# The inverse of an RWKV recurrence: two heads in one 128x128 block, or each head as its own 64x64 product

## The chip, the core and the metric

The kernel runs on one core of a Trainium2 chip. The core has TensorE (PE, matrix products into PSUM, with its weight loads shown apart as PEld), VectorE (DVE), ScalarE (ACT), GpSimd (POOL) and SyncE (SP, which issues transfers). The engines run their own instruction streams and meet at semaphores. The metric is the device time of one launch in microseconds (us), less is better.

## The reference

One inference step of a hybrid recurrent decoder in fp32: 512 prompt tokens and 8 sample tokens go through an even layer (RG-LRU and RWKV-7, dense SwiGLU, gated embedding) and an odd layer (Mamba-2 SSD and GLA, top-2-of-8 mixture of experts, gated embedding). The part that matters here is the RWKV-7 recurrence of the prompt, 8 heads of 64x64:

```
def step(S, inp):
    r_t, k_t, v_t, d_t, kk_t, a_t = inp
    S = (S * d_t[:, :, None, :]
         - einsum('bhvk,bhk->bhv', S, kk_t)[..., None] * (kk_t * a_t)[:, :, None, :]
         + v_t[..., None] * k_t[:, :, None, :])
    return S, einsum('bhvk,bhk->bhv', S, r_t)
```

## The kernel before

The step is not run token by token. The 512 tokens are cut into 8 chunks of 64. Inside a chunk each head needs the inverse of a unit lower triangular 64x64 matrix, identity plus a strictly triangular A. Heads are held in pairs: 4 pairs (t), the first head of a pair on partitions 0 to 63, the second on 64 to 127 (hh). The recurrence block (lines 655 to 876) makes four passes, s = 0 to 3, of two chunks each (cc), so that a pass inverts 8 pairs (n = 4 cc + t), 16 matrices.

Before the change a pair is one block-diagonal 128x128 matrix. AL holds A (L605), with zeros off the diagonal blocks, set once by GpSimd (L664). DD is the inverse so far, EE its transpose (DVE's transpose works in 32x32 blocks, which is enough up to the fourth level), OO the part of A that the next level takes in, GG a product on its way.

A pass has three pieces.

- Head: PE writes A by 64x64 products into the diagonal quarters of `ps0` (L740, `ab_mm`), then the products for the output (L747, into `ps1` and `ps2`), then transposes (L755, L763). DVE copies A out of PSUM (L835, two copies), masks it (L837), forms identity minus mask (L838), transposes it (L839), masks A for the first level (L842), and then masks the output products (L847, `am_read`). ScalarE copies the transposes out (L801, L805).
- Five levels l = 0 to 4, each in two groups of four pairs (cc, the chunks). PE forms G = OO' EE (L778), ScalarE copies G (L811), PE forms the correction (L784, at the last level L786), DVE subtracts it from DD (L854) and transposes DD into EE (L855); at the last level it subtracts from EE (L858) and nothing follows. GpSimd masks A for the next level (L670, `next_o`) as soon as G is out.
- The recurrence over the two chunks (`recur`, L698), small products whose first ones stand at L678 and L688. It waits for the last subtraction (`de_read`).

Of the kernel before, what the change touches and what calls it, by code (L numbers as in the profile page):

```python
# [17 lines left out]
ALU = mybir.AluOpType  # L18
# [3 lines left out]
P = 128  # L22
# [84 lines left out]
def build_program(nc, i, o):  # L107

    with ExitStack() as ctx:
# [510 lines left out]
        names = ("ab_mm", "ab_read", "am_mm", "am_read", "bk_mm", "bk_read", "v_mm", "v_read", "d_ready", "e_ready",  # L620
# [30 lines left out]
        def nth(s, l, cc):  # L651

            return 10 * s + 2 * l + cc + 1

        with nc.Block() as block:
            @block.sync
            def _(sp):
                loaded.on(sp.dma_start(Dm[:, 0:961], i["ph_rw"]), 16)  # L658

            @block.gpsimd  # L660
            def _(pool):
                S = Serial(pool, pool_step)
                pool_step.on(pool.memset(B[0:64, 10240:11264], 0.0))
                S(pool.memset(u_sb[:, 0:1024], 0.0))  # L664
                for s in range(4):
                    for l in range(4):
                        for cc in range(2):
                            n = slice(4 * cc, 4 * cc + 4)
                            w(pool, "g_mm", nth(s, l, cc))
                            g["next_o"].on(pool.tensor_tensor(OO[:, n], AL[:, n], spread(level(l + 2), 4, 1), ALU.mult))  # L670

            @block.tensor
            def _(pe):
# [24 lines left out]
                def recur(c, cc):  # L698
# [32 lines left out]
                for s in range(4):  # L731
                    if s:
                        w(pe, "de_read", 10 * s)
                        w(pe, "z_read", 4 * s)
                        w(pe, "y_read", 2 * s)
                    for cc in range(2):
                        for t in range(4):
                            n = (4 * cc + t) * P
                            for hh in range(2):
                                mm = pe.matmul(ps[0][64 * hh:64 * hh + 64, n + 64 * hh:n + 64 * hh + 64],  # L740
# [25 lines left out]
                    w(pe, "d_ready", s + 1)  # L766
                    w(pe, "am_read", 2 * s + 2)
                    w(pe, "v_read", s + 1)  # L768
                    for l in range(5):
                        for cc in range(2):  # L770
                            if l == 0:
                                w(pe, "o_ready", 2 * s + cc + 1)  # L772
                                w(pe, "e_ready", s + 1)  # L773
                            else:
                                w(pe, "next_o", 8 * s + 2 * (l - 1) + cc + 1)
                                w(pe, "de_read", nth(s, l - 1, cc))
# [3 lines left out]
                        for cc in range(2):  # L780
                            w(pe, "g_read", nth(s, l, cc))
                            for n in range(4 * cc, 4 * cc + 4):
                                if l < 4:
                                    mm = pe.matmul(ps[1][:, n * P:(n + 1) * P], GG[:, n, :], DD[:, n, :], start=True, stop=True)  # L784
                                else:
                                    mm = pe.matmul(ps[2][:, n * P:(n + 1) * P], DD[:, n, :], GG[:, n, :], start=True, stop=True)  # L786
                            g["eg_mm"].on(mm)
                    w(pe, "de_read", 10 * s + 10)
# [5 lines left out]
            def _(act):  # L794
                for s in range(4):
# [10 lines left out]
                    for l in range(5):  # L806
                        for cc in range(2):
                            w(act, "g_mm", nth(s, l, cc))
                            if l:
                                w(act, "eg_mm", nth(s, l - 1, cc))  # L810
                            g["g_read"].on(act.activation(u_sb[:, 3072 + 512 * cc:3584 + 512 * cc],  # L811
                                                          ps[0][:, 512 * cc:512 * cc + 512], ACT.Copy))
# [14 lines left out]
            def _(dve):  # L827
                S = Serial(dve, dve_step)
                dve.wait_ge(loaded.sem, loaded.count)
                dve.wait_ge(pool_step.sem, pool_step.at(2))  # L830
                for s in range(4):
                    w(dve, "ab_mm", s + 1)
                    for hh in range(2):
                        j = 64 * hh
                        S(dve.tensor_copy(AL[j:j + 64, :, j:j + 64], pairs(ps[0][j:j + 64, :])[:, :, j:j + 64]),  # L835
                          g["ab_read"] if hh else None)
                    S(dve.tensor_tensor(OO, AL, spread(level(0), 8, 1), ALU.mult))  # L837
                    S(dve.tensor_tensor(DD, spread(ident, 8, 1), OO, ALU.subtract), g["d_ready"])  # L838
                    S(dve.transpose(u_sb[:, 2048:3072], u_sb[:, 1024:2048]), g["e_ready"])  # L839
                    for cc in range(2):  # L840
                        n = slice(4 * cc, 4 * cc + 4)
                        S(dve.tensor_tensor(OO[:, n], AL[:, n], spread(level(1), 4, 1), ALU.mult), g["o_ready"])  # L842
# [6 lines left out]
                    for l in range(5):  # L849
                        for cc in range(2):  # L850
                            n, half = slice(4 * cc, 4 * cc + 4), slice(512 * cc, 512 * cc + 512)
# [1665 lines left out]
```

## Time and profile before

| | |
|---|---|
| median of 3 runs | 2316.57 us (2315.2 to 2317.98) |
| the profiled execution, its time | 2314.37 us |
| its span, first to last instruction | 2312.6 us |
| PE busy, PEld busy | 2034.9 us (88%), 1801.2 us (78%) |
| DVE, ACT, POOL busy | 648.3 us (28%), 368.1 us (16%), 154.1 us (7%) |
| mean granted clock | 0.93 of 2.4 GHz |
| recurrence block | some 185 us, from 218.8 to 404 |

The busy shares are means over the whole program. The large matrix products with streamed weights make most of it; the recurrence block is 8% of the span, and in it the shares are different, so it has to be read by itself. The granted clock is 1.00 or 0.50, that is 2.4 or 1.2 GHz; values between are means over a stretch.

### The profile page before, as it was taken

Reading aid. Unit: us, or ns where it says so; the run is one execution under the profiler, and the core shown is the slowest. Engines: PE = TensorE matmul, PEld = TensorE weight load, DVE = VectorE, ACT = ScalarE, POOL = GpSimd, SP = SyncE. Lnnn points to the kernel's source line nnn. Section 1 sums busy time; section 2 is a strip of 40 time slices with the busy share of each in tenths; the row PEclk is TensorE's granted clock in tenths of the full one; section 3 lists DMA queues with packets and bytes.
Section 4 is the critical chain, followed back from the end, with each engine's and each line's share of the span. In section 5 each row is a group of like instructions: output and inputs, shape, how many; then the busy total and the mean of one; then the engine's idle time right before and its main releaser. Section 6 shows DMA issues by size and latency. Waiting matters only on the chain. (4 is left out here: it accounts for less than half of the span.)

```text
span 2312.6 us, 31395 instructions
## 1 busy us (share of the span) xinstructions
PE 2034.9 (88%) x12810; PEld 1801.2 (78%) x12810; DVE 648.3 (28%) x991; ACT 368.1 (16%) x716; POOL 154.1 (7%) x171
## 2 busy tenths in 40 slices
PE   6987777598999999998999776859999999999677
PEld 5876666277888888876888454759999999999566
DVE  4378555722000000023620666220000000000053
ACT  1553222100000000011231111110111110111121
POOL 0001221503000000000000200010000000000100
PEclk9999999899999999999999766959999999999878
DMA  4111000118322222222222200048878878877520
GB/s 158 64 55 55 1 1 2 41 56 334 129 76 78 73 88 75 71 75 79 73 73 73 89 19 21 19 149 274 280 254 269 271 264 277 284 258 264 218 75 37
DMA packets 73824, 292.20 MB, mean 126 GB/s; under 512 B 8513, under 2 KB 9665, under 8 KB 72465
## 3 DMA queue, kind: packets, MB, share of 16 engines
q1 hardware_dynamic: 61920, 249.68, 31.8%
q0 software_dynamic: 7904, 28.46, 3.2%
q10 hardware_dynamic: 3920, 12.93, 1.6%
q8 instruction: 58, 0.95, 0.2%
q14 instruction: 22, 0.17, 0.0%
HBM read 255.50 MB, written 35.54 MB: 126 GB/s over the span
## 5 line engine op out<-in xcount | busy, mean ns | idle before, releaser
L190 PE MATMUL ps<-normed,ring 128*128 128x260 f32 (+1 forms) x3424 | 763.6, 385 | 16.7 <-DVE normed L233 16.7
L190 PEld LDWEIGHTS ps<-normed,ring 128*128 128x128 f32 (+1 forms) x3424 | 652.1, 191 | 125.4 <-issue 22.9
L2167 PE MATMUL ps<-proj,ring 128*128 128x144 f32 x3168 | 392.9, 287 | 3.5 <-DVE proj L2250 3.1
L2167 PEld LDWEIGHTS ps<-proj,ring 128*128 128x128 f32 x3168 | 391.0, 191 | 4.3 <-DVE proj L2250 3.8
L2184 PE MATMUL ps<-temps,ring 128*128 128x144 f32 x1584 | 200.5, 286 | 0.0
L2184 PEld LDWEIGHTS ps<-temps,ring 128*128 128x128 f32 x1584 | 197.2, 190 | 0.0
L190 PE MATMUL ps<-proj,ring 128*128 128x260 f32 x640 | 151.1, 397 | 18.4 <-PEq L904 8.5
L190 PEld LDWEIGHTS ps<-proj,ring 128*128 128x128 f32 x640 | 126.7, 199 | 40.9 <-issue 14.1
L190 PE MATMUL ps<-wide,ring 128*128 128x260 f32 x704 | 154.6, 383 | 0.9 <-DVE wide L1214 0.9
L190 PEld LDWEIGHTS ps<-wide,ring 128*128 128x128 f32 x704 | 133.7, 190 | 21.8 <-DVE wide L1214 1.3
L2243 DVE TENSOR_TENSOR temps<-temps,ps 128x144 f32<-128x144 f32 x99 | 30.2, 305 | 361.6 <-PE ps L2167 324.6
L1214 DVE TENSOR_TENSOR wide<-temps,ps 128x520 f32 (+1 forms) x22 | 15.3, 696 | 291.9 <-PE ps L190 291.9
L778 PE MATMUL ps<-normed,temps 128*128 128x128 f32 x320 | 50.8, 312 | 43.5 <-DVE temps L847 26.3
L778 PEld LDWEIGHTS ps<-normed,temps 128*128 128x128 f32 x320 | 44.8, 218 | 49.1 <-issue 49.1
L208 ACT ACTIVATE temps<-resid 128x520 f32<-128x520 f32 (+1 forms) x56 | 34.6, 632 | 291.6 <-DVE resid L1223 158.3
L2215 ACT ACTIVATE temps<-ps 128x144 f32<-128x144 f32 x99 | 28.8, 291 | 310.2 <-PE ps L2167 310.1
L2245 DVE COPY proj<-ps 128x512 f32<-128x512 f32 x9 | 6.2, 692 | 205.2 <-PE ps L2110 205.2
L1193 ACT ACTIVATE temps<-ps 128x520 f32<-128x520 f32 x22 | 13.3, 604 | 294.4 <-PE ps L190 294.4
L2282 POOL DMA_INDIRECT wide<-rows_y,slot_of x10 | 9.3, 934 | 645.0 <-SPq L2273 642.3
L2218 ACT ACTIVATE proj<-ps 128x144 f32<-128x144 f32 x72 | 21.0, 291 | 190.6 <-PE ps L2184 190.6
L670 POOL TENSOR_TENSOR temps<-normed,phase 128x512 f32<-128x512 f32 x32 | 40.6, 1270 | 128.0 <-PE ps L778 128.0
L190 PE MATMUL ps<-temps,consts 128*128 128x260 f32 x28 | 13.0, 609 | 38.8 <-PEq L262 15.9
(441 smaller groups left out, 1616.9 us busy)
## 6 DMA issues: line engine op xcount, KB each, us to landing
ring<-in_w_moe_gu SPq DMA_DIRECT2D x198, 512.0 KB, 4.3
ring<-in_w_moe_dn SPq DMA_DIRECT2D x72, 704.0 KB, 5.8
ring<-in_w_gu SPq DMA_DIRECT2D x44, 512.0 KB, 3.5
ring<-in_w_in_cd SPq DMA_DIRECT2D x25, 512.0 KB, 3.5
ring<-in_w_in_ab SPq DMA_DIRECT2D x22, 512.0 KB, 3.5
ring<-in_w_dn SPq DMA_DIRECT2D x16, 704.0 KB, 4.0
ring<-in_w_ple SPq DMA_DIRECT2D x16, 640.0 KB, 4.0
rows_x<-proj POOLq DMA_DIRECT2D x18, 512.0 KB, 11.1
```

The source lines that it names most:

```text
L190: mm = pe.matmul(dst[0:width, a:a + HALF], slab[:, k * width:(k + 1) * width], x[:, a:a + HALF], start=first and k == 0, stop=last and k = ...
L208: act.activation(SQ_SUM if m == 0 else sq_tmp(m), h3[:, m, :] if src is None else src, ACT.Square).then_inc(sq_done.sem, 1)
L670: g["next_o"].on(pool.tensor_tensor(OO[:, n], AL[:, n], spread(level(l + 2), 4, 1), ALU.mult))
L778: mm = pe.matmul(ps[0][:, n * P:(n + 1) * P], OO[:, n, :], EE[:, n, :], start=True, stop=True)
L1193: act.activation(tmp2(m), pt(2 * (m % 2)), ACT.Silu).then_inc(silu_done.sem, 1)
L1214: dve.tensor_tensor(dst, tmp2(m), pt(2 * (m % 2) + 1), ALU.mult).then_inc(hid_done.sem, 1)
L2167: mm = pe.matmul(hid_psum(m, s), slot(Q_MOE + 2 * m + s)[:, f * P:(f + 1) * P], XT[:, f, :], start=f == 0, stop=f == KD - 1)
L2184: mm = pe.matmul(down_psum(m), slot(Q_MOE + 2 * KE + m)[:, f * P:(f + 1) * P], HK(f), start=f == 0, stop=f == KE - 1)
L2215: act.activation(TMPH(m), hid_psum(m, 0), ACT.Silu).then_inc(silu_done.sem, 1)
L2218: act.activation(YT[:, m, :], down_psum(m), ACT.Copy).then_inc(yt_cp.sem, 1)
L2243: dve.tensor_tensor(HK(m), TMPH(m), hid_psum(m, 1), ALU.mult).then_inc(hid_done.sem, 1)
L2282: gather_in[tt].on(pool.indirect_dma_start(out=dst[0:w, :], out_offset=None, in_=rows_y[:, :], in_offset=at), 16)
```

## The change

Each head becomes a product of its own on a quarter of the array. AL, DD, EE, GG and OO hold 64 columns a pair instead of 128: head 0 on partitions 0 to 63, head 1 on 64 to 127, both in the same columns, and no zeros. `by_head` issues for each pair two 64x64 products, from partitions 0 to 63 into 0 to 63 and from 64 to 127 into 64 to 127. The masks come with 64 columns (577 columns in place of 961). The copy of A is one instruction, the memset of AL goes, and all DVE, ScalarE and GpSimd instructions on these tiles have half the columns. There are still two groups of four pairs a level (GROUPS = 2). The signal `d_ready` goes, and PE's wait for `am_read` moves behind the G products of level 0.

The diff, without the renaming of cc to gr in the waits:

```diff
-        rwmask, level = Dm[:, 0:P], lambda l: Dm[:, P * (1 + l):P * (2 + l)]
-        sign, i64 = Dm[:, 7 * P:7 * P + 1], Dm[:, 7 * P + 1:7 * P + 65]
+        rwmask, level = Dm[:, 0:P], lambda l: Dm[:, P + 64 * l:P + 64 * (l + 1)]
+        sign, i64 = Dm[:, 512:513], Dm[:, 513:577]
-        AL, DD, EE, GG = [pairs(u_sb[:, n * 1024:(n + 1) * 1024]) for n in range(4)]
-        OO = pairs(C[:, 0:1024])
+        heads = lambda ap: ap.rearrange("p (n c) -> p n c", c=64)
+        AL, DD, EE, GG = [heads(u_sb[:, n * 512:(n + 1) * 512]) for n in range(4)]
+        OO = heads(C[:, 0:512])
+        GROUPS = 2
+        PER_G = 8 // GROUPS
+        members = lambda gr: slice(PER_G * gr, PER_G * (gr + 1))
+        gcols = lambda base, gr: slice(base + 64 * PER_G * gr, base + 64 * PER_G * (gr + 1))
...
+        def nth(s, l, gr):
+
+            return GROUPS * (5 * s + l) + gr + 1
+
+        def g_psum(gr):
+            return ps[0][:, 512 * gr:512 * gr + 64 * PER_G]
+
+        def d_psum(gr, l):
+            return ps[1 if l < 4 else 2][:, 512 * gr:512 * gr + 64 * PER_G]
+
+        def by_head(pe, dst, lhs, rhs, gr):
+
+            for n in range(PER_G):
+                for hh in range(2):
+                    j = slice(64 * hh, 64 * hh + 64)
+                    mm = pe.matmul(dst[j, 64 * n:64 * n + 64], lhs[j, PER_G * gr + n, :], rhs[j, PER_G * gr + n, :],
+                                   start=True, stop=True)
+            return mm
...
-                loaded.on(sp.dma_start(Dm[:, 0:961], i["ph_rw"]), 16)
+                loaded.on(sp.dma_start(Dm[:, 0:577], i["ph_rw"]), 16)
...
-                S(pool.memset(u_sb[:, 0:1024], 0.0))
...
-                            g["next_o"].on(pool.tensor_tensor(OO[:, n], AL[:, n], spread(level(l + 2), 4, 1), ALU.mult))
+                            g["next_o"].on(pool.tensor_tensor(OO[:, n], AL[:, n], spread(level(l + 2), PER_G, 1), ALU.mult))
...
-                                               EE[j:j + 64, 4 * cc + t, j:j + 64], Qs[j:j + 64, t, :],
+                                               EE[j:j + 64, 4 * cc + t, :], Qs[j:j + 64, t, :],
...
-                                mm = pe.matmul(ps[0][64 * hh:64 * hh + 64, n + 64 * hh:n + 64 * hh + 64],
+                                mm = pe.matmul(ps[0][64 * hh:64 * hh + 64, n:n + 64],
...
-                    w(pe, "d_ready", s + 1)
-                    w(pe, "am_read", 2 * s + 2)
                     w(pe, "v_read", s + 1)
                     for l in range(5):
...
-                            for n in range(4 * cc, 4 * cc + 4):
-                                mm = pe.matmul(ps[0][:, n * P:(n + 1) * P], OO[:, n, :], EE[:, n, :], start=True, stop=True)
-                            g["g_mm"].on(mm)
...
+                            g["g_mm"].on(by_head(pe, g_psum(gr), OO, EE, gr))
+                        if l == 0:
+                            w(pe, "am_read", 2 * s + 2)
+                        for gr in range(GROUPS):
+                            w(pe, "g_read", nth(s, l, gr))
+                            lhs, rhs = (GG, DD) if l < 4 else (DD, GG)
+                            g["eg_mm"].on(by_head(pe, d_psum(gr, l), lhs, rhs, gr))
...
-                            g["g_read"].on(act.activation(u_sb[:, 3072 + 512 * cc:3584 + 512 * cc],
-                                                          ps[0][:, 512 * cc:512 * cc + 512], ACT.Copy))
+                            g["g_read"].on(act.activation(u_sb[:, gcols(1536, gr)], g_psum(gr), ACT.Copy))
...
-                dve.wait_ge(pool_step.sem, pool_step.at(2))
...
-                    for hh in range(2):
-                        j = 64 * hh
-                        S(dve.tensor_copy(AL[j:j + 64, :, j:j + 64], pairs(ps[0][j:j + 64, :])[:, :, j:j + 64]),
-                          g["ab_read"] if hh else None)
+                    S(dve.tensor_copy(AL, heads(ps[0][:, 0:512])), g["ab_read"])
                     S(dve.tensor_tensor(OO, AL, spread(level(0), 8, 1), ALU.mult))
-                    S(dve.tensor_tensor(DD, spread(ident, 8, 1), OO, ALU.subtract), g["d_ready"])
-                    S(dve.transpose(u_sb[:, 2048:3072], u_sb[:, 1024:2048]), g["e_ready"])
+                    S(dve.tensor_tensor(DD, spread(i64, 8, 1), OO, ALU.subtract))
+                    S(dve.transpose(u_sb[:, 1024:1536], u_sb[:, 512:1024]), g["e_ready"])
...
-                                S(dve.tensor_tensor(DD[:, n], DD[:, n], pairs(ps[1][:, half]), ALU.subtract))
-                                S(dve.transpose(u_sb[:, 2048 + 512 * cc:2560 + 512 * cc],
-                                                u_sb[:, 1024 + 512 * cc:1536 + 512 * cc]), g["de_read"])
+                                S(dve.tensor_tensor(DD[:, n], DD[:, n], heads(d_psum(gr, l)), ALU.subtract))
+                                S(dve.transpose(u_sb[:, gcols(1024, gr)], u_sb[:, gcols(512, gr)]), g["de_read"])
                             else:
-                                S(dve.tensor_tensor(EE[:, n], EE[:, n], pairs(ps[2][:, half]), ALU.subtract), g["de_read"])
+                                S(dve.tensor_tensor(EE[:, n], EE[:, n], heads(d_psum(gr, l)), ALU.subtract), g["de_read"])
```

What stands on PE between the head's transposes and the second level, before (`normed` holds AL, DD, EE and GG, `temps` holds OO, `wide` the chunk's operands):

```order
L763 MATMUL ps<-consts,wide 128x64 x15
L778 MATMUL ps<-normed,temps 128x128 [waits rw_o_ready,rw_v_read,rw_e_ready,rw_am_read,rw_d_ready]
L778 MATMUL ps<-normed,temps 128x128 x3
L778 MATMUL ps<-normed,temps 128x128 [waits rw_e_ready,rw_o_ready]
L778 MATMUL ps<-normed,temps 128x128 x3
L784 MATMUL ps<-normed 128x128 [waits rw_g_read]
L784 MATMUL ps<-normed 128x128 x3
L784 MATMUL ps<-normed 128x128 [waits rw_g_read]
L784 MATMUL ps<-normed 128x128 x3
L778 MATMUL ps<-normed,temps 128x128 [waits rw_de_read,rw_next_o]
```

And after the change (L671 is the product in `by_head`, L782 the same transposes as L763):

```order
L782 MATMUL ps<-consts,wide 128x64 x15
L671 MATMUL ps<-normed,temps 64x64 [waits rw_e_ready,rw_o_ready,rw_v_read]
L671 MATMUL ps<-normed,temps 64x64 x7
L671 MATMUL ps<-normed,temps 64x64 [waits rw_e_ready,rw_o_ready]
L671 MATMUL ps<-normed,temps 64x64 x7
L671 MATMUL ps<-normed 64x64 [waits rw_g_read,rw_am_read]
L671 MATMUL ps<-normed 64x64 x7
L671 MATMUL ps<-normed 64x64 [waits rw_g_read]
L671 MATMUL ps<-normed 64x64 x7
L671 MATMUL ps<-normed,temps 64x64 [waits rw_de_read,rw_next_o]
```

The wait for `am_read` has moved from the first G product to the first correction product, two groups later, and each group has 8 products instead of 4.

On DVE the head of a pass, before:

```order
L835 COPY normed<-ps 64x8x64 [waits dve_step]
L837 TENSOR_TENSOR temps<-normed,phase 128x1024 [waits rw_ab_read]
L838 TENSOR_TENSOR normed<-consts,temps 128x1024 [waits dve_step]
L839 STREAM_TRANSPOSE normed<-normed 128x1024 [waits rw_d_ready]
L842 TENSOR_TENSOR temps<-normed,phase 128x512 [waits rw_e_ready]
L842 TENSOR_TENSOR temps<-normed,phase 128x512 [waits rw_o_ready]
L847 TENSOR_TENSOR temps<-ps,phase 128x1024 [waits rw_am_mm,rw_o_ready]
L847 TENSOR_TENSOR temps<-ps,phase 128x1024 [waits rw_am_mm,rw_am_read]
L854 TENSOR_TENSOR normed<-normed,ps 128x512 [waits rw_eg_mm,rw_am_read]
```

And after:

```order
L844 COPY normed<-ps 128x512 [waits rw_ab_mm,loaded]
L845 TENSOR_TENSOR temps<-normed,phase 128x512 [waits rw_ab_read]
L846 TENSOR_TENSOR normed<-phase,temps 128x512 [waits dve_step]
L847 STREAM_TRANSPOSE normed<-normed 128x512 [waits dve_step]
L850 TENSOR_TENSOR temps<-normed,phase 128x256 [waits rw_e_ready]
L850 TENSOR_TENSOR temps<-normed,phase 128x256 [waits rw_o_ready]
L855 TENSOR_TENSOR temps<-ps,phase 128x1024 [waits rw_am_mm,rw_o_ready]
L855 TENSOR_TENSOR temps<-ps,phase 128x1024 [waits rw_am_mm,rw_am_read]
L862 TENSOR_TENSOR normed<-normed,ps 128x256 [waits rw_eg_mm,rw_am_read]
```

The order is the same but for one copy that went; the widths are halved on all but the two maskings of the output products (L847 before, L855 after).

## Rows read from the trace of the kernel before

**Rows 1.** a stage: length, busy us of PE, PEld, DVE, ACT, POOL, clock, DMA
```profile
264.50:310.00 45.50, 32.81 (x454) 30.61 (x452) 24.96 (x39) 10.40 (x23) 10.16 (x8) 0.92 0.01 1
```

**Rows 2.** timeline, head of pass s=1: start, length, engine, instruction, idle before
```profile
266.21 1.15 PE L740 MATMUL ps<-wide 64*64 64x64 f32 x32 [0.68 <-DVE phase L874]
267.46 1.41 DVE L835 COPY normed<-ps 64x512 f32<-64x512 f32 x2 [1.35 <-PE ps L740]
271.01 1.02 ACT L805 ACTIVATE wide<-ps 64x1024 f32<-64x1024 f32 x1
271.43 1.25 DVE L839 STREAM_TRANSPOSE normed<-normed 128x1024 f32<-128x1024 f32 x1
272.71 1.42 DVE L842 TENSOR_TENSOR temps<-normed,phase 128x512 f32<-128x512 f32 x2
274.16 2.48 DVE L847 TENSOR_TENSOR temps<-ps,phase 128x1024 f32<-128x1024 f32 x2
276.75 3.55 PE L778 MATMUL ps<-normed,temps 128*128 128x128 f32 x16 [6.41 <-DVE temps L847]
281.29 0.69 DVE L854 TENSOR_TENSOR normed<-normed,ps 128x512 f32<-128x512 f32 x1 [4.65 <-PE ps L784]
```

**Rows 3.** timeline, one level of pass s=0
```profile
238.63 0.71 DVE L855 STREAM_TRANSPOSE normed<-normed 128x512 f32<-128x512 f32 x1
239.46 0.97 PEld L778 LDWEIGHTS ps<-normed,temps 128*128 128x128 f32 x8 [0.50 <-issue]
240.34 1.93 PEld L784 LDWEIGHTS ps<-normed 128*128 128x128 f32 x16
241.62 0.69 DVE L854 TENSOR_TENSOR normed<-normed,ps 128x512 f32<-128x512 f32 x1 [2.28 <-PE ps L784]
242.34 0.71 DVE L855 STREAM_TRANSPOSE normed<-normed 128x512 f32<-128x512 f32 x1
```

**Rows 4.** timeline, tail of pass s=0
```profile
257.14 0.69 DVE L858 TENSOR_TENSOR normed<-normed,ps 128x512 f32<-128x512 f32 x1 [2.28 <-PE ps L786]
258.84 0.69 PE L678 MATMUL ps<-wide,temps 128*64 128x64 f32 x16 [0.85 <-DVE normed L858]
```

**Rows 5.** groups by shape: count, busy us, mean ns, idle before; then two timeline rows
```profile
L740 PE MATMUL ps<-wide 64*64 64x64 f32 x128 | 5.4, 243 | 6.3 <-PEq L362 4.3 <-DVE phase L874 2.0
L740 PEld LDWEIGHTS ps<-wide 64*64 64x64 f32 x128 | 4.9, 156 | 7.0 <-issue 7.0
L873 DVE TENSOR_TENSOR phase<-ps,phase 128x128 f32<-128x128 f32 x14 | 4.1, 292 | 9.3 <-PE ps L720 9.0
L855 DVE STREAM_TRANSPOSE normed<-normed 128x512 f32<-128x512 f32 x32 | 22.8, 711 | 1.1
L823 ACT ACTIVATE proj<-ps 128x256 f32<-128x256 f32 x8 | 3.1, 384 | 8.1 <-PE ps L725 8.1
L670 POOL TENSOR_TENSOR temps<-normed,phase 128x512 f32<-128x512 f32 x32 | 40.6, 1270 | 128.0 <-PE ps L778 128.0
...
262.38 0.68 PE L688 MATMUL ps<-phase,wide 64*64 64x64 f32 x16
262.83 0.55 PEld L695 LDWEIGHTS ps<-wide,phase 64*64 64x64 f32 x16
```

**Rows 6.** timeline, head of pass s=0
```profile
218.90 1.97 PE L740 MATMUL ps<-wide 64*64 64x64 f32 x32 [4.28 <-PEq L362]
222.17 1.41 DVE L835 COPY normed<-ps 64x512 f32<-64x512 f32 x2 [3.82 <-DMA phase<-in_ph_rw]
236.44 0.69 DVE L854 TENSOR_TENSOR normed<-normed,ps 128x512 f32<-128x512 f32 x1 [5.09 <-PE ps L784]
```

**Rows 7.** granted clock of short stretches, and PE around its fall at 416
```profile
272.00:274.00 2.00, 0.00 (x0) 0.00 (x0) 1.93 (x3) 0.03 (x1) 0.00 (x0) 0.78 0.00 0
416.70:418.40 1.70, 1.70 (x4) 0.67 (x3) 1.31 (x2) 0.95 (x2) 0.00 (x0) 0.50 0.00 0
...
415.55 5.40 PE L921 MATMUL ps<-normed,consts 128*128 128x512 f32 x8 [2.17 <-POOL normed L979]
```

More of the change, by code:

```diff
@@ L618, in rk @@
             return B[64 * hh:64 * hh + 64, j:j + 64 * n]
-        names = ("ab_mm", "ab_read", "am_mm", "am_read", "bk_mm", "bk_read", "v_mm", "v_read", "d_ready", "e_ready",
+        names = ("ab_mm", "ab_read", "am_mm", "am_read", "bk_mm", "bk_read", "v_mm", "v_read", "e_ready",
                  "o_ready", "next_o", "g_mm", "g_read", "eg_mm", "de_read", "q_mm", "q_read", "p_mm",
@@ L663, in _ @@
                 pool_step.on(pool.memset(B[0:64, 10240:11264], 0.0))
-                S(pool.memset(u_sb[:, 0:1024], 0.0))
                 for s in range(4):
                     for l in range(4):
-                        for cc in range(2):
-                            n = slice(4 * cc, 4 * cc + 4)
-                            w(pool, "g_mm", nth(s, l, cc))
-                            g["next_o"].on(pool.tensor_tensor(OO[:, n], AL[:, n], spread(level(l + 2), 4, 1), ALU.mult))
+                        for gr in range(GROUPS):
+                            n = members(gr)
+                            w(pool, "g_mm", nth(s, l, gr))
+                            g["next_o"].on(pool.tensor_tensor(OO[:, n], AL[:, n], spread(level(l + 2), PER_G, 1), ALU.mult))
             @block.tensor
@@ L732, in _ @@
                     if s:
-                        w(pe, "de_read", 10 * s)
+                        w(pe, "de_read", 5 * GROUPS * s)
                         w(pe, "z_read", 4 * s)
@@ L806, in _ @@
                     for l in range(5):
-                        for cc in range(2):
-                            w(act, "g_mm", nth(s, l, cc))
+                        for gr in range(GROUPS):
+                            w(act, "g_mm", nth(s, l, gr))
                             if l:
-                                w(act, "eg_mm", nth(s, l - 1, cc))
-                            g["g_read"].on(act.activation(u_sb[:, 3072 + 512 * cc:3584 + 512 * cc],
-                                                          ps[0][:, 512 * cc:512 * cc + 512], ACT.Copy))
+                                w(act, "eg_mm", nth(s, l - 1, gr))
+                            g["g_read"].on(act.activation(u_sb[:, gcols(1536, gr)], g_psum(gr), ACT.Copy))
                     for cc in range(2):
@@ L849, in _ @@
                     for l in range(5):
[L850 to L852 removed]
+                        for gr in range(GROUPS):
+                            n = members(gr)
+                            w(dve, "eg_mm", nth(s, l, gr))
                             if l < 4:
[L854 to L856 removed]
+                                S(dve.tensor_tensor(DD[:, n], DD[:, n], heads(d_psum(gr, l)), ALU.subtract))
+                                S(dve.transpose(u_sb[:, gcols(1024, gr)], u_sb[:, gcols(512, gr)]), g["de_read"])
                             else:
[L858 removed]
+                                S(dve.tensor_tensor(EE[:, n], EE[:, n], heads(d_psum(gr, l)), ALU.subtract), g["de_read"])
                     for cc in range(2):
@@ L2378, in shape_constants @@
         ti, si = r[:, None], r[None, :]
-        levels.append(((ti // (2 * m) == si // (2 * m)) & ((ti // m) % 2 == 1) & ((si // m) % 2 == 0)).astype(np.float32))
+        levels.append(((ti // (2 * m) == si // (2 * m)) & ((ti // m) % 2 == 1) & ((si // m) % 2 == 0)).astype(np.float32)[:, 0:64])
+        levels[-1][64:] = levels[-1][:64]
     sign = np.where(np.arange(P) < 64, -1.0, 1.0).astype(np.float32)[:, None]
```

30 lines of the change are left out of this document (10 added, 20 removed).

## The prediction

> **What bounds the kernel now.** I first read the busy time by stage [rows 1]. The RWKV recurrence runs as four passes (s = 0 to 3) of some 45.5 us each. In the second, TensorE (PE) works 32.8 us and VectorE (DVE) 25.0 us out of 45.5: neither is full, so the stage is a chain that goes back and forth between them, and an instruction only counts if it lies on that chain. The timeline shows the chain in three pieces.
>
> The head of a pass [rows 2]: PE starts its small products at 266.21, DVE can start at 267.46, and from there it works without a hole: two copies out of PSUM (1.41), a mask and identity minus mask (from 268.87 to 271.43, 1.28 each with their gaps), transpose (1.25), two masks (1.42), two maskings of the 1024-wide products (2.48). The first inverse product waits for the last of them (releaser DVE L847) and starts at 276.75. The first subtraction L854 comes at 281.29, 13.83 after DVE's start.
>
> One level [rows 3]: the second group's transpose ends at 239.34, PE loads that group's G product at 239.46 (0.12 later), starts the first group's EG product at 240.34 (0.88 later), DVE subtracts at 241.62 (1.28 later: the product's end and a handover of 0.05), then four DVE operations (0.69, 0.71, 0.69, 0.71 and three gaps of 0.03) end 2.89 later, and the next level's second G product follows. 0.12 + 0.88 + 1.28 + 2.89 = 5.17, which is the distance of two levels: the first subtractions stand at 236.44 [rows 6] and 241.62, 5.18 apart. ScalarE's copy of G and GpSimd's mask are done earlier and only have to keep up.
>
> The tail [rows 4]: from the last level's first subtraction (257.14) to the recurrence's first product (258.84) 1.70.
>
> **The change, part by part.** Every operation of the inverse works on 64 columns a head pair instead of 128. What each costs:
>
> DVE, rows of before at several widths: an operation of this kind out of PSUM takes 292 ns at 128 columns [rows 5] and 0.69 us at 512 [rows 3], so 1.04 ns a column and 0.43 at 256. A transpose takes 0.711 at 512 [rows 5] and 1.25 at 1024 [rows 2], so 0.44 at 256 on the same line. A mask at 512 takes 0.69 (two with a gap 1.42 [rows 2]). The copy of AL is one in place of two (0.70 instead of 1.41). Bounds: no 256-wide operation of these kinds is in the trace; half of the 512-wide time (0.34 and 0.36) is the least, the full 512-wide time the most; I take the line, since two points support it. Four operations with three gaps of 0.03 then last 0.43 + 0.44 + 0.43 + 0.44 + 0.09 = 1.83, not 2.89.
>
> ScalarE: a 128x256 copy out of PSUM is in the trace, 384 ns [rows 5]. GpSimd: 1270 ns at 512 [rows 5]; at 256 it lies between half and all of that. Even at all of it two masks (2.5 us) fit into the level of 3.15 worked out below; at the 0.9 that I expect there is 1 us to spare.
>
> PE: a group is no longer 4 products of 128x128 on the whole array (8 records) but 8 of 64x64, alternating between two opposite quarters (16 records). The trace has exactly this form: L740, with the same two quarters, into one bank, 32 records in 1.15 at the full clock [rows 2]. Two such groups of 16 records in the recurrence start 0.46 apart (262.38, 262.83) and one needs 0.68 to its end [rows 5]. So a group takes 0.46 to issue (was 0.88) and 0.69 + 0.05 from its first load to DVE's start (was 1.28).
>
> Whether the two quarters really overlap decides this price. If they took turns, a record would cost half of a full 128-column one, 0.88 / 8 / 2 = 55 ns; L740 shows 1.15 / 32 = 36 ns at most, and the recurrence 0.46 / 16 = 29 ns. I take 29 and keep 55 as a rival. The Trainium skill, "TensorEngine Tiling (Array Packing)", section "Restrictions and Gotchas", says that different row tiles cannot use one PSUM bank at the same time; both row halves write one bank here, so by that rule they would take turns, and the trace does not agree for this diagonal pair of quarters.
>
> One level is then 0.12 + 0.46 + 0.74 + 1.83 = 3.15. EG waits for nothing new: the first group's G starts 0.81 before the second's transpose ends, is out 0.12 before that end, and its copy ends 0.30 after it, while EG is issued 0.58 after it. Saved: 5.17 - 3.15 = 2.02 a level, four levels a pass, 8.08.
>
> Head: DVE's row from its start to am_read is 0.70 + 0.69 + 0.69 + 0.71 + 2 x 0.43 + 2.48 + 6 x 0.03 = 6.31. The wait for am_read now stands behind the first G products, so these run under DVE's two large maskings. They wait for ScalarE's copy of v (L805, ends 272.03 [rows 2]) and would start at 272.15; both copies of G are out by 273.8, about when am_read comes (267.46 + 6.31 = 273.77). Then 0.11 and 0.74 to the first subtraction: 7.16 in place of 13.83, saved 6.67. This move is where I cost the G products of level 0 and their copies at nothing: the maskings hide them; without that cover they would cost 1.2. The same two maskings (2.48) are late next, unchanged by this edit.
>
> Tail: the second EG group starts when its G is copied, 1.28 in my count from the transpose's end, is out at 2.02, subtracted at 2.45; the recurrence starts at 2.56, 1.24 after the first subtraction (1.32). Saved 1.70 - 1.24 = 0.46.
>
> First pass: DVE starts at 222.17 on the table's transfer and subtracts at 236.44 [rows 6], 14.27 later; 7.16 saves 7.11. The table shrinks from 961 to 577 columns; DVE can start no sooner than L740's end (218.90 + 1.97 = 220.87), so the gain is between 0 and 1.25; I take 0.7, by the 40% fewer bytes. GpSimd's memset of 1024 columns goes, for nothing: it ended before DVE's start.
>
> Sum: three passes at 6.67 + 8.08 + 0.46 = 15.21 are 45.6, the first 7.11 + 0.7 + 8.08 + 0.46 = 16.35: 62.0 saved.
>
> **The clock.** Ahead of L778 at 276.75 PE was idle for 6.41 [rows 2]; the granted clock fell from 2.4 to 1.2 GHz in that wait (0.78 in the stretch 272 to 274, so at about 273.1 [rows 7]), and the first 16 records took 3.55, where 16 at the full clock are loaded in 1.93 [rows 3]. That loss sits in the head that the change shortens, where PE's wait shrinks from 6.41 to some 1.8 us (it ends at 272.15 instead of 276.75). But a wait of 2.17 behind L979 was also followed by a fall: 0.50 in the stretch 416.7 to 418.4 [rows 7]. So some passes will still see 1.2 GHz after the head. Price: L740 at half clock takes 1.97 for 1.15 [rows 2, 6], a group 0.36 more to issue and about 0.5 more to its end: 0.87 more a level, and two levels and a little run so, some 2.2. Of the four passes I count one to two: 3 us.
>
> The profiled execution took 2314.37, its span 2312.6, so 1.8 lies around it, unchanged. 2314.37 - 62.0 + 3 = 2255.4. The median of the runs shown, 2316.57, is 2.2 higher; I lean a little to it: **2256**.
>
> **Rivals.**
> (A) The forecast, 2249 to 2262: 0.70.
> (B) The new products run slower in every level: they take turns (55 ns a record), or the clock does not hold at 2.4 GHz under products on quarters. Both give a group of some 0.88: level 0.12 + 0.88 + 1.15 + 1.83 = 4.0, 0.85 more in each of 16 levels, 3 more in heads and tails: 2252.4 + 13.6 + 3 = 2269. Against: L740, and the recurrence, which runs on quarters at full clock. For: PE's waits between groups are a larger share of 3.15 than of the recurrence. 0.12.
> (C) DVE's operations do not shrink with the columns: at the 512-wide time a level is 3.15 + 1.06, 17 us in all, 2271. For: no 256-wide row. Against: the line through other widths. 0.05.
> (D) The gain is given back downstream: the next block starts earlier and waits there. Its transfers are issued in the block itself, and weights come through a ring that moves with PE, so I find no fixed time to wait for; 2275 to 2316. 0.04. That it is all given back, so no change: 0.01 of it.
> (E) More is saved: no falls of the clock, smaller DVE times, down to 2245: 0.06.
> (F) Slower than before. Each quarter's weight load waits for the other quarter's product to end, since the array changes tile at every instruction: a load (156 ns) and a product (243 ns) one behind the other [rows 5] are 0.40 a record, 6.4 a group, 5.7 more. Ten groups a pass lie in series (one in the head, two a level, one in the tail), 40 x 5.7 = 228: 2252 + 228 = 2480. It decides from 62 / 40 = 1.55 more a group, some 126 ns a record; L740 shows at most 36. 0.03.
>
> About 0.2% (5 us) is what a measurement of this kernel can tell from no change. Faster: A, B, C, E and most of D, 0.96; same 0.01; slower 0.03. The range 2247 to 2268 holds A, nearly all of E and part of B.
>
> **What would show it.** Level to level, the first subtractions 3.15 apart (4.0 under B or C; then PE's record spacing or DVE's durations tell which). The first subtraction 7.2 after DVE's AL copy. DVE TENSOR_TENSOR at 128x256 0.42 and transpose 0.44, ScalarE 0.38, GpSimd under 1.27. Groups of 16 records in 0.55 of loads. Granted clock 1.00 in most of the levels. The passes some 30 us apart instead of 45.3. If the L854-like subtraction waits for GpSimd's mask or for ScalarE's copy instead, my chain is wrong.

## The result and the profile after

The changed kernel takes 2257.34 us (median of 4, 2255.17 to 2259.21), the kernel before in the same runs 2317.28 (2315.20 to 2318.14). The ratio is 0.9742, 95% interval 0.9725 to 0.9759. The prediction was 2256, range 2247 to 2268. The profiled execution took 2255.17 against 2314.37, its span is 2253.3 against 2312.6.

All of the 59.3 us of the span lies in the recurrence block. It lasted from the first A product to the next block's first transfer 404.17 - 218.90 = 185.27; now 344.80 - 219.44 = 125.36, 59.9 less. It starts 0.5 later, and what follows it lasts 1908.4 before and 1908.5 now. The busy times of the second pass, from the view by stage, in the columns of [rows 1]:

```profile
250.90:282.70 31.80, 25.44 (x608) 23.14 (x608) 17.33 (x38) 8.25 (x22) 5.77 (x8) 0.89 0.01 2
```

The pass is 31.8 long instead of 45.5 (from the first copy of one pass to that of the next the passes take 30.2, 31.8 and 30.6; the profile of before has 45.3, 45.5 and 46.5); PE gave up 7.4 of busy time and DVE 7.6, so most of what a pass lost was chain, not the work of one engine.

The head of that pass, from the timeline, against [rows 2]:

```profile
250.99 1.15 PE L759 MATMUL ps<-wide 64*64 64x64 f32 x32 [0.68 <-DVE phase L881]
...
252.25 0.69 DVE L844 COPY normed<-ps 128x512 f32<-128x512 f32 x1 [1.36 <-PE ps L759]
...
255.17 0.89 DVE L850 TENSOR_TENSOR temps<-normed,phase 128x256 f32<-128x256 f32 x2
255.80 1.02 ACT L818 ACTIVATE wide<-ps 64x1024 f32<-64x1024 f32 x1
256.09 2.48 DVE L855 TENSOR_TENSOR temps<-ps,phase 128x1024 f32<-128x1024 f32 x2
...
256.87 1.15 PE L671 MATMUL ps<-normed,temps 64*64 64x64 f32 x32 [1.75 <-ACT wide L818]
...
258.63 1.97 PE L671 MATMUL ps<-normed 64*64 64x64 f32 x32 [0.61 <-DVE temps L855]
...
259.86 0.42 DVE L862 TENSOR_TENSOR normed<-normed,ps 128x256 f32<-128x256 f32 x1 [1.29 <-PE ps L671]
...
263.92 0.42 DVE L862 TENSOR_TENSOR normed<-normed,ps 128x256 f32<-128x256 f32 x1 [2.23 <-PE ps L671]
```

The G products start at 256.87 on ScalarE's copy of v, while DVE still masks; the correction products start at 258.63 when DVE is done. The 32 records of G take 1.15, the 32 of the correction 1.97: the clock fell between them, and the next first subtraction comes 4.06 later instead of the 3.24 of a level at the full clock.

One level at the full clock, in the first pass, against [rows 3], and the tail of that pass against [rows 4]:

```profile
230.88 0.45 DVE L863 STREAM_TRANSPOSE normed<-normed 128x256 f32<-128x256 f32 x1
...
231.45 0.57 PEld L671 LDWEIGHTS ps<-normed,temps 64*64 64x64 f32 x16 [0.36 <-issue]
...
231.91 1.27 PEld L671 LDWEIGHTS ps<-normed 64*64 64x64 f32 x32
...
232.73 0.42 DVE L862 TENSOR_TENSOR normed<-normed,ps 128x256 f32<-128x256 f32 x1 [1.40 <-PE ps L671]
...
235.97 0.42 DVE L862 TENSOR_TENSOR normed<-normed,ps 128x256 f32<-128x256 f32 x1 [1.40 <-PE ps L671]
...
242.44 0.42 DVE L865 TENSOR_TENSOR normed<-normed,ps 128x256 f32<-128x256 f32 x1 [1.40 <-PE ps L671]
...
243.62 0.69 PE L697 MATMUL ps<-wide,temps 128*64 128x64 f32 x16 [0.59 <-DVE normed L865]
```

Transpose ends 231.33, load 231.45 (0.12), next group 231.91 (0.46), first subtraction 232.73 (0.82), and DVE's four operations end 1.84 after that: 3.24 a level, and the next first subtraction stands at 235.97. The tail is 1.18. The groups by shape (mean ns behind the busy time), against [rows 5]:

```profile
L689 POOL TENSOR_TENSOR temps<-normed,phase 128x256 f32<-128x256 f32 x32 | 23.1, 726 | 88.8 <-PE ps L671 88.6
L824 ACT ACTIVATE normed<-ps 128x256 f32<-128x256 f32 x40 | 15.3, 384 | 47.5 <-PE ps L671 47.2
L863 DVE STREAM_TRANSPOSE normed<-normed 128x256 f32<-128x256 f32 x32 | 14.2, 445 | 1.1
L862 DVE TENSOR_TENSOR normed<-normed,ps 128x256 f32<-128x256 f32 x32 | 13.5, 421 | 22.7 <-PE ps L671 22.2
```

### The profile page after: what moved, and what is told of

It is laid out like the page before. It is cut to its first block and busy times, and to the rows that moved or that the text cites. A ratio compares the mean times of both kernels' runs of the same rounds, so it can differ in the third digit from the quotient of the medians.

```text
span 2253.3 us, 32669 instructions
## 1 busy us (share of the span) xinstructions
PE 1998.1 (89%) x13450; PEld 1763.9 (78%) x13450; DVE 617.9 (27%) x987; ACT 359.3 (16%) x716; POOL 135.9 (6%) x170
## 5 line engine op out<-in xcount | busy, mean ns | idle before, releaser
L1230 DVE TENSOR_TENSOR resid<-ps,resid 128x520 f32 (+1 forms) x8 | 5.6, 700 | 146.8 <-PE ps L190 146.8
L671 PE MATMUL ps<-normed,temps 64*64 64x64 f32 x640 | 27.6, 230 | 18.2 <-DVE normed L863 11.2
L671 PEld LDWEIGHTS ps<-normed,temps 64*64 64x64 f32 x640 | 23.6, 141 | 22.3 <-issue 14.7
```

The source lines that it names most:

```text
L671: mm = pe.matmul(dst[j, 64 * n:64 * n + 64], lhs[j, PER_G * gr + n, :], rhs[j, PER_G * gr + n, :], start=True, stop=True)
```

## The experiments

The theory is the chain account of the prediction: head, levels and tail, each the sum of PE's groups and DVE's operations on the way. The rivals are that one engine's part makes the whole gain; that the move of the wait is worth nothing; that the quarters do not overlap, or cost the clock. Each kernel ran in three rounds beside the kernel before. The block's length, read as above in each kernel's profiled execution, takes out what happens elsewhere. The last column is the distance of two levels' first subtractions while the clock is at 2.4 GHz.

| kernel | median us | ratio to before (95%) | block us | level, full clock |
|---|---|---|---|---|
| before | 2317.28 | 1 | 185.3 | 5.17 |
| changed | 2257.34 | 0.9742 (0.9725 to 0.9759) | 125.4 | 3.24 |
| E1 wait back in front | 2261.44 | 0.9767 (0.9751 to 0.9784) | 131.1 | 3.24 |
| E2 before, wait moved | 2302.76 | 0.9946 (0.9929 to 0.9962) | 173.5 | 5.17 |
| E3 quarter after quarter | 2269.72 | 0.9805 (0.9789 to 0.9821) | 138.1 | 3.60 |
| E4 one group a level | 2313.03 | 0.9986 (0.9976 to 0.9995) | 181.5 | not seen |
| E5 before, products on quarters | 2305.21 | 0.9958 (0.9944 to 0.9972) | 173.4 | 4.30 |
| E6 shorter head | 2250.76 | 0.9716 (0.9700 to 0.9732) | 119.4 | 3.24 |
| E7 before, half the products | 2370.92 | 1.0237 (1.0220 to 1.0255), see below | 172.8 | 4.28 to 4.29 |
| E8 products twice | 2277.43 | 0.9831 (0.9814 to 0.9847) | 144.1 | 4.17 |
| E9 maskings in the levels | 2247.09 | 0.9704 (0.9688 to 0.9720) | 117.4 | 3.24 |

### E1 and E2: what the move of the wait is worth

```diff
+                    w(pe, "am_read", 2 * s + 2)
                     w(pe, "v_read", s + 1)
                     for l in range(5):
...
-                        if l == 0:
-                            w(pe, "am_read", 2 * s + 2)
```

> The changed kernel, with PE's wait for am_read put back ahead of the G products of level 0. Theory (the wait's move pays because DVE's two large maskings hide the first G products and their copies): the first subtraction comes 6.31 + 0.11 + 1.16 (G product, copy, handovers) + 0.82 = 8.40 after DVE's AL copy starts instead of 7.18, 1.2 more a pass, 4.9 in all; PE's wait grows to 3.5 us, so the granted clock falls in more passes, 0 to 4 us more. 2262 to 2266. Rival (the G products are hidden anyway, the move is worth nothing): no change, 2257.

```profile
261.49 1.97 PE L671 MATMUL ps<-normed,temps 64*64 64x64 f32 x32 [3.51 <-DVE temps L854]
```

E2 is the opposite edit in the kernel before.

> The kernel before, with the wait for am_read moved behind the G products of level 0 and nothing else. Theory: the first G products start some 3.2 us sooner, at half clock since PE has been idle, and the first correction product starts when am_read comes, so the first subtraction is 2.0 to 3.0 sooner in each pass: 8 to 12 us less, 2306 to 2309. Rival (most of the gain of the head comes from halved columns, the move alone gives nothing): 2317.

E1's median is 4.1 above the changed kernel's, by the ratios 5.8, and its block is 5.7 longer. The first subtraction comes 8.75 to 9.32 after the AL copy, against 7.18 to 7.63. That is more than the 8.40 expected: PE now waits 3.51 in three of the four heads (the row above is from the second), and in every head one set of 32 records takes 1.92 to 1.97 where it takes 1.15 at the full clock. The rival of no change is out. The median came just under the stated 2262 to 2266.

E2 took 2302.76, 12.6 us less than the kernel before beside it and less than the 2306 to 2309 expected. Its head (pass s=1):

```profile
265.78 1.41 DVE L836 COPY normed<-ps 64x512 f32<-64x512 f32 x2 [1.36 <-PE ps L740]
...
271.98 3.50 PE L777 MATMUL ps<-normed,temps 128*128 128x128 f32 x16 [3.32 <-DVE temps L843]
...
275.27 2.14 PE L785 MATMUL ps<-normed 128*128 128x128 f32 x16
...
276.63 0.69 DVE L855 TENSOR_TENSOR normed<-normed,ps 128x512 f32<-128x512 f32 x1 [1.67 <-PE ps L785]
```

G starts at 271.98, 6.20 after the copy where it was 9.29 in [rows 2], so 3.0 of its 3.50, at half clock, run under the maskings (to 274.96), and the corrections behind it already run at the full clock (2.14 for 16 records and their end). The first subtraction comes after 10.85 instead of 13.83. So the wait alone, in the old widths, is worth a fifth of the whole gain. In the new widths it is worth 4 to 6 us: there G takes 1.15 and not 3.50, so there is less to hide. The parts do not simply add.

### E3: do the two quarters overlap?

```diff
-            for n in range(PER_G):
-                for hh in range(2):
+            for hh in range(2):
+                for n in range(PER_G):
```

> The changed kernel, but a group's 8 products run first all four in one quarter, then all four in the other, instead of alternating. Theory (the quarters overlap when they alternate; a record alone takes half of a full one, 55 ns): a group takes 0.88 instead of 0.46 to issue and 0.42 more to its end, a level 3.24 + 0.84 = 4.08, 13.4 us in 16 levels and 2 more in heads and tails: 2273. Rival (records are bound by issue at 29 ns whatever quarter they use): no change, 2257.

```profile
234.93 0.42 DVE L862 TENSOR_TENSOR normed<-normed,ps 128x256 f32<-128x256 f32 x1 [1.76 <-PE ps L671]
...
237.46 0.19 PEld L671 LDWEIGHTS ps<-normed 64*64 64x64 f32 x2
...
237.51 0.14 PEld L671 LDWEIGHTS ps<-normed,temps 64*64 64x64 f32 x1
...
237.57 0.14 PEld L671 LDWEIGHTS ps<-normed 64*64 64x64 f32 x1
...
237.63 1.52 PEld L671 LDWEIGHTS ps<-normed 64*64 64x64 f32 x29
...
238.53 0.42 DVE L862 TENSOR_TENSOR normed<-normed,ps 128x256 f32<-128x256 f32 x1 [1.76 <-PE ps L671]
```

In this timeline the last 29 loads of a level take 1.52, 52 ns each, changes of quarter among them. A short window on the loads of one quarter shows what a record costs there alone:

```profile
236.94 0.25 PEld L671 LDWEIGHTS ps<-normed,temps 64*64 64x64 f32 x3
```

Three loads of 0.135 each span 0.25, so they start 58 ns apart; the prediction put 55 on this. The 29 of the changed kernel is overlap, and the rival of an issue limit is out.

But a level became 3.60, not 4.08. The rows at 237.46 to 237.57 show why: the correction group's first records (one quarter) start between the last records of the second G group (the other quarter). The same happens at the change of quarter inside a group, which is why the 29 loads come to 52 ns each and not 58. So the records need not alternate one by one to overlap; a change of quarter every 8 records hid some three of them. The second G group was 0.57 ahead of the corrections instead of 0.46, and those took 1.07 to the subtraction instead of 0.82, which makes the 0.36. The section on the kernel before says that nothing reorders what PE runs; across two quarters the records do not start strictly in the written order.

The median, 2269.72, is under the 2273 expected. It is 12.4 above the changed kernel's (by the ratios 14.6), part of it from falls of the clock in all four passes: three first levels took 4.80 and the first head 9.27.

### E5 and E8: PE's part and DVE's part

E5 puts only the products on quarters, inside the old 128-wide tiles:

```diff
-                            for n in range(4 * cc, 4 * cc + 4):
-                                mm = pe.matmul(ps[0][:, n * P:(n + 1) * P], OO[:, n, :], EE[:, n, :], start=True, stop=True)
+                            mm = by_head(pe, ps[0], OO, EE, cc)
...
+            for n in range(4 * cc, 4 * cc + 4):
+                for hh in range(2):
+                    j = slice(64 * hh, 64 * hh + 64)
+                    k = slice(n * P + 64 * hh, n * P + 64 * hh + 64)
+                    mm = pe.matmul(dst[j, k], lhs[j, n, j], rhs[j, n, j], start=True, stop=True)
```

> The kernel before, with its 128-column tiles, widths of DVE, ScalarE and GpSimd and its wait for am_read, but the inverse's products issued as 64x64 products on the two diagonal quarters (the other two quarters of each block are not computed, and are not used). Theory (a level is the chain 0.12 + issue of G + EG to its end + DVE's four operations): 0.12 + 0.46 + 0.82 + 2.89 = 4.29 instead of 5.17, 14 us in 16 levels, and 1.3 a pass in the head: 19 to 20 less, 2297. Rival (the gain of the change is all DVE's columns, PE's products lie beside it): 2317. Rival (it is all PE's): 2257.

```profile
283.76 0.69 DVE L859 TENSOR_TENSOR normed<-normed,ps 128x512 f32<-128x512 f32 x1 [2.22 <-PE ps L661]
...
285.34 0.68 PE L661 MATMUL ps<-normed,temps 64*64 64x64 f32 x16 [0.79 <-DVE normed L860]
...
286.81 0.68 PE L661 MATMUL ps<-normed,temps 64*64 64x64 f32 x16 [0.78 <-DVE normed L860]
...
288.07 0.69 DVE L859 TENSOR_TENSOR normed<-normed,ps 128x512 f32<-128x512 f32 x1 [1.40 <-PE ps L661]
...
291.12 1.07 PE L661 MATMUL ps<-normed,temps 64*64 64x64 f32 x16 [0.79 <-DVE normed L860]
...
291.92 2.07 PE L661 MATMUL ps<-normed 64*64 64x64 f32 x32
...
293.15 0.69 DVE L859 TENSOR_TENSOR normed<-normed,ps 128x512 f32<-128x512 f32 x1 [2.18 <-PE ps L661]
```

At the full clock the level is 4.30 to 4.31 (283.76 to 288.07), as computed (4.29). The very next one takes 5.08: the group of 16 that took 0.68 takes 1.07. In this kernel the clock fell again and again inside the levels, and half of the expected 20 us was lost: 10 remain in the medians (2305.21 beside 2315.34, where 2297 was expected) and 12 in the block. The sum of the chain was right, and both rivals, 2317 and 2257, are out; what the expectation left out was the clock.

E8 is the other half, the changed kernel with every group issued twice, so that a group costs PE 0.92 to issue (0.88 before the change):

```diff
-            for n in range(PER_G):
+            for n in [n for _ in range(2) for n in range(PER_G)]:
```

> The changed kernel with every group of the inverse's products issued twice over (the second time with the same result), so that PE's groups cost what they cost before (0.92 to issue) while DVE, ScalarE and GpSimd keep half the columns. Theory (chain): a level is 0.12 + 0.92 + 1.28 + 1.84 = 4.16 instead of 3.24, 14.7 us in 16 levels, 4 more in heads and tails: 2274 to 2278. Rival (with DVE's columns halved PE's products hide beside it): 2257 to 2260.

```profile
237.23 0.42 DVE L862 TENSOR_TENSOR normed<-normed,ps 128x256 f32<-128x256 f32 x1 [2.33 <-PE ps L671]
...
241.40 0.42 DVE L862 TENSOR_TENSOR normed<-normed,ps 128x256 f32<-128x256 f32 x1 [2.33 <-PE ps L671]
```

The time is 2277.43 and a level 4.17 (first subtractions at 237.23 and 241.40), both as computed; in its last three passes the clock did not fall once. So with PE's cost near the old one, the narrower tiles and the moved wait are worth 39 us, and PE's cheaper products give the other 20. Taken alone in the old kernel they gave 10 to 12, because there the clock fell in the levels. Of the 39, the wait is worth what E1 and E2 show; how the rest divides among the widths of DVE, ScalarE and GpSimd no run shows.

### E4 and E7: why the clock fell

```diff
-        GROUPS = 2
+        GROUPS = 1
```

> The changed kernel with GROUPS = 1: all 8 pairs of a level in one group, so DVE, ScalarE and GpSimd have half the instructions at twice the width and nothing overlaps inside a level. Theory (a level is a chain): 0.12 + 1.19 (G) + 0.60 (copy) + 0.05 + 1.20 (EG) + 1.43 (subtraction and transpose at 512) = 4.59 instead of 3.24, 21.6 in 16 levels, some 0 to 2 more in heads and tails: 2279. Rival (fixed costs of the many small instructions bound a level, so fewer are as good): 2250 to 2260.

```profile
280.85 1.67 PE L671 MATMUL ps<-normed 64*64 64x64 f32 x32 [0.69 <-ACT normed L824]
...
295.29 0.69 DVE L862 TENSOR_TENSOR normed<-normed,ps 128x512 f32<-128x512 f32 x1 [4.90 <-PE ps L671]
...
296.87 1.98 PE L671 MATMUL ps<-normed,temps 64*64 64x64 f32 x32 [1.70 <-DVE normed L863]
298.88 0.60 ACT L824 ACTIVATE normed<-ps 128x512 f32<-128x512 f32 x1 [5.74 <-PE ps L671]
...
299.53 1.97 PE L671 MATMUL ps<-normed 64*64 64x64 f32 x32 [0.69 <-ACT normed L824]
301.62 0.69 DVE L865 TENSOR_TENSOR normed<-normed,ps 128x512 f32<-128x512 f32 x1 [4.90 <-PE ps L671]
```

The expectation was 2279, the kernel took 2313: neither theory nor rival. Nearly all levels stand at 6.33, not 4.59. Each group of 32 records takes 1.98 where it takes 1.15 at the full clock, so 1.7 of the 1.74 missing is half clock. In the first pass the clock fell in the head. In the other three it fell within the first level, which took 5.17 to 5.19; in the first of these three the G group still took 1.15 and the correction group 1.67, and without the 0.52 that it lost the level is 4.67, near the 4.59 computed. Each time the clock came back only with the recurrence. In every level PE had waits of 1.70 and 0.69.

Either these waits are the reason, or products on quarters hold the clock less than full ones (a rival of the prediction). The changed kernel and E8 have the same products on quarters as E4 and held the clock in nearly all levels. E7 puts the question to E5: the kernel before with two of the four products of a group, on the full array, so that the timing is E5's. PE is busy for 117.3 us of the block, in E5 for 116.9.

```diff
-                            for n in range(4 * cc, 4 * cc + 4):
+                            for n in range(4 * cc, 4 * cc + 2):
...
-                                S(dve.tensor_tensor(DD[:, n], DD[:, n], pairs(ps[1][:, half]), ALU.subtract))
+                                S(dve.tensor_tensor(twice(DD, n), twice(DD, n), spread(pairs(ps[1][:, 512 * cc:512 * cc + 256]), 2, 1),
+                                                    ALU.subtract))
```

> The kernel before, with only the first two of the four pairs of each group multiplied on the full array; the other two pairs are corrected with those results, so that the output is not the reference's. A group is 4 records of 128x128 that last as long as e5's 16 records of 64x64, so all engines have the same timing as in e5_quarters_only and differ only in how much of the array works. Open since e5 and e4: there the clock fell again and again within the levels, and in the changed kernel it did not. Theory 1 (what counts is how long PE has work, not how much of the array): the clock falls within the levels as in e5, levels of 4.3 and 5.1 mixed, 2302 to 2308. Theory 2 (products on quarters hold the clock less than full ones): the clock holds after the head, all levels 4.3, 2294 to 2299.

```profile
238.75 0.68 PE L780 MATMUL ps<-normed,temps 128*128 128x128 f32 x4 [0.78 <-DVE normed L858]
...
240.17 0.69 DVE L856 TENSOR_TENSOR normed<-normed,ps 128x512 f32<-128x512 f32 x1 [1.56 <-PE ps L786]
...
243.22 1.19 PE L780 MATMUL ps<-normed,temps 128*128 128x128 f32 x4 [0.28 <-DVE normed L858]
...
245.37 0.69 DVE L856 TENSOR_TENSOR normed<-normed,ps 128x512 f32<-128x512 f32 x1 [2.30 <-PE ps L786]
```

Its total, expected at 2302 to 2308, says nothing, since other values go into the mixture of experts behind the block and change the routing there (220 transfers of `in_w_moe_gu` instead of 198); only the block is compared. It lasts 172.8, E5's 173.4, and the clock falls in it in the same way: a group takes 0.68 and soon after 1.19, levels of 4.3 and 5.2 are mixed, and the mean granted clock of the block is 0.78, in E5 0.77, in the kernel before 0.92. With equal timing, full products lost the clock as quarters did, so the quarters are not what E5 lost it by. For E4, whose waits are longer still, no such twin with full products was run; there the waits are the reading that is left, not one that a run isolates.

### E6 and E9: a shorter head

The profile after shows what is late next in the head: ScalarE's copy of v for G, DVE's maskings for the corrections. In E6 PE transposes v ahead of bk, ScalarE copies v first and bk after level 0's copies, and the second masking moves:

```diff
                             g["g_read"].on(act.activation(u_sb[:, gcols(1536, gr)], g_psum(gr), ACT.Copy))
+                        if l == 0:
+                            w(act, "bk_mm", s + 1)
...
+                            g["bk_read"].on(act.activation(C[:, 3072:4096], ps[3][:, :], ACT.Copy, scale=sign))
...
-                    for cc in range(2):
+                    for cc in range(1):
                         w(dve, "am_mm", 2 * s + cc + 1)
...
                     for l in range(5):
+                        if l == 1:
+                            cc = 1
+                            w(dve, "am_mm", 2 * s + cc + 1)
```

> The changed kernel with a shorter head: PE does the transposes of v before those of bk, ScalarE copies v first and bk only after the copies of level 0, and DVE's masking of the second output product (1.23) moves out of the head into DVE's idle 1.40 between level 0 and level 1. Theory (the head is DVE's row up to the first masking, then 0.82): the first subtraction 7.18 - 1.2 = 6.0 after the AL copy, 1.2 less a pass, 4.8 in all, and PE's wait shrinks to about 1 us, so no fall of the clock in the passes, 1 to 3 us more: 2249 to 2252. Rival (the masking does not fit into the idle time and pushes level 1): the gain is eaten, 2255 to 2258.

E9 puts the corrections into the free columns of ps0, so that the inverse does not need ps1 and ps2 and both maskings can move; PE's wait for `am_read` goes behind the levels. Against E6:

```diff
-            return ps[1 if l < 4 else 2][:, 512 * gr:512 * gr + 64 * PER_G]
+            return ps[0][:, 512 * gr + 256:512 * gr + 256 + 64 * PER_G]
...
-                        if l == 1:
-                            cc = 1
+                        if l in (1, 2):
+                            cc = l - 1
```

> The kernel of e6_head_short, with the correction products put into the unused columns of ps0 so that ps1 and ps2 are not needed by the inverse, and both maskings of the output products moved into DVE's idle time after levels 0 and 1. Theory: the first G products wait for ScalarE's copy of v, the first subtraction comes 5.5 after the AL copy instead of 5.92, 0.4 a pass, 1.6 in all: 2248 to 2250. Rival (the correction products now share a bank with the G products that ScalarE reads, and wait or disturb): 2251 to 2260.

```profile
251.49 0.69 DVE L844 COPY normed<-ps 128x512 f32<-128x512 f32 x1 [1.35 <-PE ps L759]
...
253.90 1.02 ACT L811 ACTIVATE wide<-ps 64x1024 f32<-64x1024 f32 x1 [3.91 <-PE ps L775]
...
254.98 1.15 PE L671 MATMUL ps<-normed,temps 64*64 64x64 f32 x32 [0.62 <-ACT wide L811]
...
256.94 0.42 DVE L863 TENSOR_TENSOR normed<-normed,ps 128x256 f32<-128x256 f32 x1 [1.64 <-PE ps L671]
...
258.81 1.22 DVE L857 TENSOR_TENSOR temps<-ps,phase 128x1024 f32<-128x1024 f32 x1
...
260.18 0.42 DVE L863 TENSOR_TENSOR normed<-normed,ps 128x256 f32<-128x256 f32 x1
```

E6: first subtraction 5.92 after the copy in three passes, median 2250.76, in the range expected. E9: 5.45, median 2247.09, 10 us better than the changed kernel (by the ratios 9) and just under the 2248 to 2250 expected. In this head PE's wait before G is 0.62 instead of 1.75. DVE's masking starts at 258.81 and ends at 260.03, the next subtraction is at 260.18, 3.24 after the last first one: the level pays nothing. In neither kernel did the clock fall in the last three passes. The rival that the shared bank or the full gap would cost time is out. E9's gain over E6 (3.7 in the medians, 2.0 in the block) is a little more than the 1.6 expected.

## Why the prediction was right, step by step

- **Levels.** Forecast 3.15, measured 3.24. 0.12, 0.46 and DVE's 1.84 were right; the correction group's end, put at 0.74 from a group that starts with PE idle, took 0.82 behind another group; that is the term that was mis-sized. From the first level's first subtraction to the last level's, the four passes saved 82.8 - 52.6 = 30.2, not 32.3: 1.3 by the 0.08 in sixteen levels, 0.8 by one level at half clock.
- **Head.** The first subtraction came 7.42, 7.61, 7.18 and 7.63 after DVE's AL copy, forecast 7.16. G started 4.62 after the copy and PE waited 1.75 for it, forecast 4.69 and 1.8. The four savings sum to 27.0, forecast 27.1, and that close is luck: two heads paid 0.43 and 0.45 for the clock, the first 0.24 to ScalarE (its copy of v ended at 227.40, after products at half clock, so that G's copy and not DVE's masking was last), and against this the kernel before had a third pass of 14.85, 1.0 longer than the one I worked from.
- **Tail.** 1.18 for 1.24; the four saved 2.1, forecast 1.8. **Table.** DVE started 0.6 sooner behind PE's first product, forecast 0.7.
- **Widths.** 421 and 445 ns for the forecast 0.43 and 0.44; ScalarE 384; GpSimd 726, where I expected 900.
- **Sum.** 62.0 less 3 for the clock was 59.0; the block gave 59.9. The clock's 3 was the loosest term: the profile shows about 1.7 (one level at 0.82, two heads at 0.45). I had taken two slow levels in a pass with a fall, and it was one at most. That 59.0 came so near 59.9 is partly luck: levels forecast 1.3 too fast stand against 1.3 too much for the clock, and the third head of before gave 1.0 that no term held. The mechanism, the chain and its waits, was as forecast but for ScalarE's copy in the first head.
- **Rivals.** B failed on both legs: quarters overlap (a group of 16 records issued in 0.46, and E3), and the clock held in fifteen of sixteen levels; at E5's timing full products hold it no better (E7). But its price was real for a near neighbour: in E4 and E5 PE waits longer between its groups, and most of E4's levels and many of E5's run at half clock. I had put 0.12 on it for the changed kernel and nothing on how near it was. C and F were out with the first rows of after, D with the 1908.4 and 1908.5 behind the block.

The Trainium skill, "TensorEngine Tiling (Array Packing)", section "Restrictions and Gotchas", says that different row tiles cannot access one PSUM bank at the same time. The traces do not agree for this diagonal pair of quarters: the two write different partitions of one bank at 29 ns a record, and a quarter alone takes 58 (E3).

## What to carry to other kernels

Where two engines hand work back and forth, write one period of the chain as a sum of handovers, issue times and durations, check it against the period before, and then put in the new durations: here it gave 3.15 for 3.24. Such a chain also sets how long PE waits, and a version that saves PE's work but not the waits (E5), or saves instructions but loses the overlap (E4), can lose to the clock what it gains. In this case a block-diagonal product was cheaper by half as separate products on opposite quarters of the array (0.46 for 0.88 a group); two thirds of the gain came with the other part, the narrower instructions of the other engines and the moved wait (E8). And a wait should stand in front of the first product that needs it, not in front of products that do not (E1, E2).

## What was not expected of the hardware

- Records of opposite quarters overlapped at every change of quarter, inside a group and over the border of two groups (E3, level 3.60 where 4.08 was computed for quarters that take turns).
- The clock stayed at 1.2 GHz through all four level-to-level steps of E4's first pass, 6.33 us each, in which PE worked 3.95 and waited 1.70 and 0.69. With the same timing it made no difference whether the products filled the array or two quarters of it (blocks of 173.4 and 172.8 us, E5 and E7). The changed kernel, with waits of 0.47 and 0.25 between its groups, held 2.4 GHz in fifteen of sixteen such steps.
